# Moving 46 of 128 down products of an expert mixer into the routing and gates stages of one Trainium2 kernel

## What is computed

```python
def _peer(h, w_query, sub_keys, expert_down, expert_up):
    q = (xt @ w_query).reshape(T, PEER_HEADS, 2, D_HALF)
    s = jnp.einsum('thpd,hpnd->thpn', q, sub_keys)
    top_s, top_i = lax.top_k(s, PEER_TOPK)
    cand = (top_s[:, :, 0, :, None] + top_s[:, :, 1, None, :]).reshape(...)
    best_s, best_c = lax.top_k(cand, PEER_TOPK)
    ...
    ids = (i1 * N_KEYS + i2);  gates = softmax(best_s)
    a = einsum('tkd,td->tk', expert_down[idb], xb)
    act = gelu(a) * gb
    return einsum('tk,tkd->td', act, expert_up[idb])
```

## Time and profile before

| what | us |
|---|---|
| median of 3 runs (1690.55 to 1692.72) | 1691.19 |
| the profiled execution's own time | 1692.26 |
| its span, first to last instruction | 1690.5 |
| token mixer, up to the first scores | 0 to 265 |
| routing heads | 265 to 434.4 |
| from there to ACT's first copy of gates | 434.4 to 453.8 |
| gates, ACT's first to last copy | 453.8 to 588.6 |
| tile loop, up to PE's last matmul | 588.6 to 1665.3 |
| rest of the fourth block, normalisation, output | 1665.3 to 1690.5 |

### The profile page before, as it was taken

The page is one execution under the profiler, slowest core; times in us unless marked ns, Lnnn a source line. Parts: engine busy times, 40 slices in busy tenths (PEclk is TensorE's granted clock), DMA queues, the critical chain, the costliest instruction groups (busy, mean ns, idle before and its releaser), DMA issues.

```text
span 1690.5 us, 25887 instructions
## 1 busy us (share of the span) xinstructions
PE 1524.0 (90%) x7686; PEld 1298.7 (77%) x7686; DVE 1196.7 (71%) x2424; ACT 661.7 (39%) x1018; POOL 721.4 (43%) x715
## 2 busy tenths in 40 slices
PE   4999989665388779999999999999999999999995
PEld 3475547554266679999999999999999999999994
DVE  6545437999799728777777777777777777777776
ACT  1124324333499923333333333333333333333332
POOL 0000004555599717544444444444444444444441
PEclk9999999887699989999999999999999999999998
DMA  9942201110016799877777787887777777777762
GB/s 325 372 168 100 76 24 50 39 48 13 0 48 178 235 306 363 323 273 272 274 272 279 277 278 278 278 278 273 280 272 273 274 277 277 281 276 278 278 247 100
DMA packets 186503, 372.36 MB, mean 220 GB/s; under 512 B 19752, under 2 KB 103280, under 8 KB 186480
## 3 DMA queue, kind: packets, MB, share of 16 engines
q1 hardware_dynamic: 149088, 237.57, 42.1%
q0 software_dynamic: 36864, 134.23, 21.8%
q10 hardware_dynamic: 528, 0.26, 0.1%
HBM read 344.76 MB, written 27.26 MB: 220 GB/s over the span
## 4 chain that ended last, share of the span: by engine, by line
PE 65%; DVE 8%; issue 4%; ACT 4%; SPq 1%; DMA 1%; POOL 0%; ACTq 0%; DVEq 0%; POOLq 0%
PE bank L1482 10%; PE bank L1484 10%; PE bank L1483 10%; PE bank L1494 10%; PE bank L1495 10%; PE bank L1493 10%; PE bank L1463 3%; ACT stage L766 2%; DVE topi L1030 1%; SPq L406 1%; DVE top L1027 1%; DVE cand L1052 1%; DVE pick L1045 1%; DVE score L1034 1%; ACT onehot L757 1%
## 5 line engine op out<-in xcount | busy, mean ns | idle before, releaser
L1482 PE MATMUL bank<-h2hi,dhi 128*128 128x384 f32 x1024 | 347.2, 339 | 13.7 <-DVE dlo L1135 13.7
L1484 PE MATMUL bank<-h2hi,dlo 128*128 128x384 f32 x1024 | 346.8, 339 | 0.0
L1483 PE MATMUL bank<-h2lo,dhi 128*128 128x384 f32 x1024 | 346.2, 338 | 0.0
L1495 PE MATMUL bank<-uhi,alo 128*128 128x512 f32 x768 | 301.3, 392 | 0.0
L1494 PE MATMUL bank<-ulo,ahi 128*128 128x512 f32 x768 | 301.0, 392 | 0.0
L1493 PE MATMUL bank<-uhi,ahi 128*128 128x512 f32 x768 | 298.6, 389 | 0.0
L543 POOL COPY idx_u<-ids 128x1 uint32 (+1 forms) x128 | 112.6, 880 | 344.8 <-DVE y L1156 344.7
L1166 DVE TENSOR_TENSOR acts<-gel,gate 128x384 f32<-128x384 f32 x128 | 71.5, 558 | 257.4 <-ACT gel L793 232.0
L545 POOL DMA_INDIRECT rows_u<-in_peer_up,idx_u x128 | 200.5, 1567 | 99.0 <-POOL idx_u L543 99.0
L1482 PEld LDWEIGHTS bank<-h2hi,dhi 128*128 128x128 f32 x1024 | 195.0, 190 | 19.5 <-DVE dlo L1135 9.8
L1483 PEld LDWEIGHTS bank<-h2lo,dhi 128*128 128x128 f32 x1024 | 194.8, 190 | 4.8
(11 more groups left out here) (202 smaller groups left out, 2281.2 us busy)
## 6 DMA issues: line engine op xcount, KB each, us to landing
down<-in_down_t SPq DMA_DIRECT2D x128, 512.0 KB
up<-in_peer_up SPq DMA_DIRECT2D x128, 512.0 KB
ada<-in_w_ada SPq DMA_DIRECT2D x12, 2048.0 KB, 16.3
gate<-gates_dram SPq DMA_DIRECT2D x128, 192.0 KB
gates_dram<-stage SPq DMA_DIRECT2D x2, 8192.0 KB, 30.4
wq<-in_peer_query SPq DMA_DIRECT2D x16, 512.0 KB, 4.0
gates_dram<-stage SPq DMA_DIRECT2D x4, 2048.0 KB, 14.5
w_in_sb<-in_w_in SPq DMA_DIRECT2D x2, 2048.0 KB, 20.1
```

The costliest lines, as they stand in the source:

```text
L1482: pe.matmul(bank[s][:, 0:TD], dhi[s][:, k, :], h2hi[:, k, 0:TD], start=k == 0, stop=False)
L1483: pe.matmul(bank[s][:, 0:TD], dhi[s][:, k, :], h2lo[:, k, 0:TD], start=False, stop=False)
L1484: last = pe.matmul(bank[s][:, 0:TD], dlo[s][:, k, :], h2hi[:, k, 0:TD], start=False, stop=k == KT - 1)
L1495: done = pe.matmul(got[:], alo[s][:, tokens], uhi[s][:, half], start=False, stop=last)
```

## The change

Tiles 0 to 45 (EARLY = 46) have their down product and gelu done ahead of the loop: two in each of heads 1 to 7, eight between the heads and the gates (four ahead of the transposes of the picks, four behind), and one in each of the 24 turns of the gates. Each gelu goes to DRAM (`gel_dram`, 192 KB) and comes back when the tile's up product is due. The loop then has 41 rounds of two down and three up products. With this come smaller edits: the keys are transposed on the host, so that PE's transposes and ACT's copies of them are gone; `stage` holds 64 tokens instead of 128, so a gate store has runs of 256 B, and there are six of them of 4 MB; the gathers have three buffers instead of four; all up products of a round have buffers of their own (SLOTS = 3).

```diff
+PER_HEAD, BETWEEN, TURNS = 2, 6, TD // (2 * TB)
+IN_HEADS = PER_HEAD * PH
+FIRST_G = IN_HEADS + BETWEEN
+EARLY = FIRST_G + TURNS
+ROUNDS = (TILES - EARLY) // 2
+CHUNK_T = 64
+CHUNKS = TD // CHUNK_T
+TURNS_C = CHUNK_T // (2 * TB)
+SLOTS = 3
@@ SP
-            sp.dma_start(keys[:], keys_v).then_inc(keys_in, 16)
+            sp.dma_start(keysT[:], keys_t).then_inc(keys_in, 16)
+            def store_gel(n, s):
+                sp.wait_ge(act_gelu, n + 1)
+                sp.dma_start(one(gel_dram, n), gel[s][:]).then_inc(gel_out[s], 16)
+
+            def next_down(n, s):
+                sp.wait_ge(dve_dlo, n + 1)
+                load_down(n + 2, s)
+            with sp.Fori(2, PH) as h:
+                next_wq(h)
+                for s in range(2):
+                    next_down(2 * h - 4 + s, s)
+                    store_gel(2 * h - 4 + s, s)
-            for b in range(GB - 1):
-                sp.wait_ge(act_g, (b + 1) * (P // 4))
-                store_block(b, slice(0, KEYS), stored[b % 2])
+            for w in range(CHUNKS):
+                with sp.Fori(0, TURNS_C // 2) as i:
+                    for s in range(2):
+                        next_down(FIRST_G + TURNS_C * w + 2 * i + s, s)
+                        store_gel(FIRST_G + TURNS_C * w + 2 * i + s, s)
+                sp.wait_ge(act_g, (w + 1) * (CHUNK_T // 4))
+                if w < CHUNKS - 1:
+                    store_chunk(w, slice(0, KEYS), stored[w % 2])
+            store_chunk(CHUNKS - 1, slice(0, 16), stored_part[0])
+            store_chunk(CHUNKS - 1, slice(EARLY, EARLY + 16), stored_part[0])
+            store_chunk(CHUNKS - 1, slice(16, EARLY), stored_part[1])
+            store_chunk(CHUNKS - 1, slice(EARLY + 16, KEYS), stored_part[1])
             for s in range(2):
+                sp.wait_ge(gel_out[s], 16 * (EARLY // 2))
+            load_gel(0, 0)
+            sp.wait_ge(stored[0], 16 * (CHUNKS // 2))
+            sp.wait_ge(stored[1], 16 * (CHUNKS // 2 - 1))
+            sp.wait_ge(stored_part[0], 32)
+            for j, n in enumerate((0, EARLY, EARLY + 1)):
+                load_gate(n, j)
@@ ACT
+            def early_gelu(n, s, first=False):
+                act.wait_ge(pe_d, n + 1)
+                if not first:
+                    act.wait_ge(gel_out[s], 8 * (n - s))
+                act.activation(gel[s][:], bank[7 * s][:, 0:TD], ACT.Gelu).then_inc(act_gelu, 1)
+
+            def early(n, s, first=False):
+                early_gelu(n, s, first=first)
+                down_hi(n + 2, s)
+            def gates_turn(w, i, e, last=False):
+                for u in range(2):
+                    gates_out(w, i, u)
+                    if not last:
+                        hot_rows(2 * (TURNS_C * w + i) + u + 2, u)
+                early(FIRST_G + TURNS_C * w + i, e)
@@ DVE
             def halves(h):
                 for s in range(2):
+                    down_lo(2 * h + s, s)
                     ve.wait_ge(act_sc, 2 * h + s + 1)
+            def round_(r, first=False, downs=True):
+                a = EARLY + 2 * r
+                fused_activations(a, 1, r)
+                if downs:
+                    down_lo(a + 2, 0)
+                loaded_activations(0, r + 1, r + 2)
+                gathered(r, 0, first=first)
+                parts_lo(0, r + 1)
+                fused_activations(a + 1, 2, r)
+                if downs:
+                    down_lo(a + 3, 1)
+                gathered(r, 1, first=first)
+                parts_lo(1, r)
+                gathered(r, 2, first=first)
+                parts_lo(2, r)
@@ PE
-                if b in (1, 2):
-                    transpose_keys(2 * b - 2)
-                    transpose_keys(2 * b - 1)
+            def head(h, first=False):
+                for s in range(2):
+                    queries(h, (s,))
+                    multiply_down(2 * h - 2 + s, s, first=first)
                 scores_of(h, (0, 1))
+            for n in range(IN_HEADS - 2, IN_HEADS + 2):
+                multiply_down(n, n % 2)
+            for n in range(IN_HEADS + 2, FIRST_G):
+                multiply_down(n, n % 2)
+            def gates_turn(t, e, first=False):
                 for u in range(2):
-                    gate_products(2 * i + u, u)
+                    gate_products(2 * t + u, u, first=first)
+                multiply_down(FIRST_G + t, e)
+            def round_(r, first=False):
+                a = EARLY + 2 * r
+                multiply_down(a, 0)
+                if first:
+                    pe.wait_ge(act_g, TD // 4)
+                multiply_up(0, r, first=first)
+                multiply_down(a + 1, 1)
+                if not first:
+                    for j in range(1, SLOTS):
+                        multiply_up(j, r - 1)
```

More of the change, by code:

```diff
@@ L730, in _ @@
             for s in range(2):
+                down_hi(s, s, first=True)
+            for s in range(2):
                 queries_out(0, (s,), first=True)
@@ L806, in _ @@
[L806 to L816 removed]
+            for n in range(IN_HEADS + 2, FIRST_G):
+                early(n, n % 2)
@@ L1198, in residual @@
+            ve.wait_ge(dve_coef, ROUNDS + 2)
+            for k in range(left):
+                add_up(PICKS - left + k, k, ROUNDS + 1)
             def residual(b, normed):
@@ L1496, in multiply_up @@
+                    pe.matmul(got[:], ahi[j][:, tokens], ulo[j][:, half], start=False, stop=False)
+                    done = pe.matmul(got[:], alo[j][:, tokens], uhi[j][:, half], start=False, stop=last)
                     if last:
```

576 lines of the change are left out of this document (325 added, 251 removed).

## The result

The changed kernel takes 1679.9 us (median of four runs, 1677.9 to 1681.2) against 1691.5 us (1690.6 to 1692.7) for the kernel before: a ratio of 0.993, interval 0.9913 to 0.9947, 11.6 us less. The forecast was 1662 us, 29 us less. The profiled execution has a span of 1679.4 us; by the sum it was to be 1661.0.

The account below looks back on a forecast made before the run. Bounds: DVE in the heads, ACT in the gates, PE in the tile loop. Terms -2 + 25.5 + 14 + 32 + 85 + 2 - 174 - 12 = -29.5 us, from 1691.2 to 1662 us; own range 1638 to 1690, chance 0.60.

Parts of the forecast that it names:

- Heads: In the heads, added down products and `dlo` cost +25.5 us; later heads come 24.4 us apart.
- the 296 among the signs: In the list of what would show it: first scores of head 1 near 296 us.
- Between: Between heads and gates, down products 18 to 21 put the first gate copy at 33.4 us against 19.4: +14.
- Gates: In the gates: ACT's added work +32 us, five waits for loads behind stores +85, PE's lower clock +2.
- S: Time of one 4.19 MB gate store in runs of 256 B, put at 19.3 us from loads at 217 GB/s.
- The rival of a dear store: Gate stores: a run of 256 B costs what one of 512 B does, 28.9 us a store; 1720 us, chance 0.20.
- that of loads passing the store: In the gates, loads share engines with the store and don't wait for it; 1575 us, chance 0.10.
- Start of the loop: Loads queue behind the last gate store, so the first up product starts 26.9 us after the gates.
- Rounds and PE's restart ahead of them: In the loop, PE's rounds take 20.75 us with transfers hidden, products 867.2 us in all; the restart costs 2.3.
- The rival of a DMA-bound loop: In the loop, transfers carry only 290 GB/s, so 278 MB take 960 us, +93: 1755 us, chance 0.10.
- End of the loop: Seven up products lack down products beside them; DVE's 4.7 us each against 4.13 starts the last 6.5 us late.
- Tail: Behind PE's last product, 13 us are left instead of 25.2, as sums to `y` are done earlier: -12.

Follow-up runs that it names:

- the second store: Changed kernel with the first five gate chunks stored again to an unread tensor: 1775.7 us in runs of 256 B, 1731.0 us in runs of 32 KB.
- the run in quarters: Changed kernel with each gate chunk's store issued in four parts of 32 keys, three of them behind loads of the next turns: 1609.2 us.
- the spread store: Changed kernel with 96 of 128 keys of the last chunk's store issued in six parts behind the first six rounds' loads: 1666.4 us.
- the run on older rows: Changed kernel without the gathers of the last five picks, the same DVE and ACT instructions working on earlier picks' rows: 1674.8 us.
- The second order: Changed kernel with low parts of the last four up products one by one between the picks, no pick moved behind a load: 1676.0 us.
- the first order of the end: Changed kernel with low and high parts of the last four up products made ahead of the last picks where possible: 1683.4 us.
- the run with the moved low parts: Changed kernel with a head's two `dlo` made later, behind the sums' first instructions and behind the last select: 1678.6 us.

## Why the prediction was right in its mechanisms and wrong in its size

The side and the range held, and nearly every mechanism came as forecast; the sum promised 18.4 us too much. By stages (miss as measured minus forecast):

- **Heads: +2.5.** Head 1's scores start at 291.62, which is the 291.5 of the sum (284.02 - 2 + 9.5); the 296 among the signs does not follow from it. Then DVE's heads come 24.5 us apart (313.91, 338.38) instead of 24.4, and the last pair is ready at 460.4 instead of 457.9. The 24.4 was right by luck. The step said that 13 `dlo` of 1.225 us come on top; in fact each from head 2's on costs 2.9 us beside POOL (head 1's two took 1.23 and 1.39), and the sums behind them, which had been held up by POOL before (3.37 us for the three of head 1, now 0.61), no longer are. The "0 to 1 us a head" that was put on POOL was too little and the sum was saved by what it gave back. Head 1 came out 2.8 us shorter than forecast, heads 2 to 5 as forecast, and the last two, in which POOL has no or fewer weights to split and which used to be 2 to 3 us shorter than the others, took 24.4 us each, together 5.3 us more than forecast.
- **Between: +2.4.** 35.8 us from the last pair to ACT's first copy of gates, forecast 33.4. Here, too, two `dlo` stand beside POOL's hits: 4.08 us instead of 2.45, 1.6 of the 2.4.
- **Gates: +1.3**, 255.1 us against 253.8. The largest term, called the least sure, was the best: S is 19.0 by the second store (19.3, taken from loads; that a store in such runs goes at their rate was a choice between two rows, and it held), five waits of 16.2 to 17.2 us against 17, a clock of 0.87 behind a chunk. The rival of a dear store (28.9) and that of loads passing the store are both ruled out, by the waits and by the run in quarters.
- **Start of the loop: +3.8.** 30.7 us from the gates' end to the first up product, forecast 26.9. The store went out 2.4 us behind ACT's last copy instead of 0.9, since the store of the last gelu, which waits for PE, is ahead of it; SP pushed the loads of gates 21.3 us behind the store where S + 0.75 was put; and from there to the product it was 7.0 us instead of 5.9.
- **Rounds and PE's restart ahead of them: +2.0.** A round takes 20.81 us instead of 20.75, since two up products behind each other take 8.35 us and not twice 4.13; over 40 rounds that is 2.4 us, and the restart took 0.4 less than its 2.3. PE has no idle time, and DMA carries 315 GB/s where 321 was worked out. The rival of a DMA-bound loop is ruled out up to the spread store, where 353 GB/s at a share of 1.00 were still hidden.
- **End of the loop: +7.1.** This is the step that failed, and the largest of the misses. It said that seven up products with a pick each set DVE's pace at 4.7 us against 4.13 and the last one starts 6.5 us late, and, one sentence before, that three gather buffers "still leave over 9 us". The 9 us hold in a round. At the end there are no down products, the last five picks follow close on one another, POOL can start their gathers of up rows only 4.7 to 6.0 us apart, and DVE's low parts stand behind the sums that wait for them. So the gathers, put at nothing, cost PE 6.8 us of waits by the run on older rows, and DVE's work 4.9 where 6.5 was put: 11.7 us, 5.2 more than the sum has. Most of the other 1.9 is the restart after the wait of 8.4 us, where PE's matmuls first start 0.43 us apart instead of 0.23. The second order, which moves no work, gave 3.9 us of it back.
- **Tail: -0.6.** 12.4 us behind the start of PE's last matmuls, forecast 13. The sums ended 6 to 7 us ahead of PE, as said ("some 5 us"), and yet their chain of 18.7 us was the one that ended last, which the step had not weighed.

Together 18.5 us, against 18.4 between the two spans. The forecast's own range, 1638 to 1690, held the result. Its list of what would make it fall named POOL holding DVE up by over 2 us a head; this was the case (two times 1.7 us), and the stage held all the same, because of the sums.

The larger point is the sum as it stood: 85 + 19 of its terms were waits for one queue, which it took for a price of the change. The quarters, with the same transfers, took 71 us of them away and the spread store 14, each measured by itself.

## What to carry to other kernels

A load that is wanted soon should never be issued behind a store of megabytes in the same queue: cut the store into parts that fit the slack of a turn and put each *behind* a load. Before a term of "hidden" gathers or loads is set to nothing, the same count has to be made for the first and last rounds, where the work that hides them is missing. Two engines that end together (here PE's products and the sums of picks) must both be followed, since taking all waits from the one may lengthen the other, as the first order of the end did. The engine that fetches for them belongs in the count: here POOL, with two gathers for each pick.

## What the hardware showed unexpectedly

- DVE's subtraction of 128x1024 takes 1.23 us alone and 2.9 to 3.4 us while POOL executes its instructions on tiles of the same size; POOL's own `hit` instructions took 1.94 us each alone (the run with the moved low parts) and 2.42 beside it. POOL's two of 1.94 us and DVE's 1.23 are 5.1 us one behind the other; together they took from 313.81 to 318.62, 4.8.
  This is a rule of the Trainium skill (SBUF — State Buffer, SBUF: two separate sides): a DVE instruction with two SBUF inputs and one of POOL that reads SBUF hold a shared pair of ports in turn, each for its whole length. The trace agrees to within 0.3 us.
- A store of 4.19 MB took 19.0 us in runs of 256 B (221 GB/s) and 9.7 us in runs of 32 KB, 431 GB/s, both by the growth of the waits, one execution each; the rounds carried 353 at a share of 1.00. In the earlier trace rows stores in runs of 512 B went at 290 GB/s. The Trainium skill (DMA: Bandwidth & Descriptors, Specifications) has read-modify-write below 512 B; here a store of 16,384 runs of 256 B landed in 21.1 us and one of as many runs of 512 B in 30.4, so halving the run saved a third of the time. The rule, read as a price for each run, would have it save none; the trace does not agree with that reading, and no run shows how the engines write such a run.
